# Product matmuls that read their moving rows alternately from two halves, in a fp32 decoder trunk

## What is computed

```python
def _swiglu(h, w_gate, w_up, w_down):
    return (jax.nn.silu(h @ w_gate) * (h @ w_up)) @ w_down

def _shortconv_mixer(h, w_in, conv_w, w_out):
    proj = h @ w_in
    b_gate, c_gate, u = jnp.split(proj, 3, axis=-1)
    z = c_gate * u
    ...
    return (b_gate * y) @ w_out

def reference(x, ...):
    for i in range(DEPTH):
        j = i // N_MIXERS
        if i % N_MIXERS == 0:
            x = x + _dsa_mixer(_rmsnorm(x, attn_norm[j]), ...)
        else:
            x = x + _shortconv_mixer(_rmsnorm(x, conv_norm[j]), ...)
        x = x + _swiglu(_rmsnorm(x, ffn_norm[i]), w_gate[i], w_up[i], w_down[i])
    return x
```

## Time and profile before

| | us |
|---|---|
| median of two runs | 2096.52 (2096.46 to 2096.58) |
| span of the profiled execution | 2096.4 |
| TensorE busy | 2081.3 (99%) |
| weight loads busy | 1729.7 (83%) |
| VectorE busy | 1725.3 (82%) |
| ScalarE busy | 1177.2 (56%) |

### The profile page before, as it was taken

How to read it: one execution, slowest core, us unless ns; L and a number is a source line. 1 busy time by engine, 2 the same in 40 slices (tenths; PEclk the granted TensorE clock), 3 DMA queues, 4 the chain that set the end, 5 groups by cost and what they waited for, 6 DMA issues and landing times.

```text
span 2096.4 us, 28772 instructions
## 1 busy us (share of the span) xinstructions
PE 2081.3 (99%) x9675; PEld 1729.7 (83%) x9675; DVE 1725.3 (82%) x1968; ACT 1177.2 (56%) x1428; POOL 118.3 (6%) x131
## 2 busy tenths in 40 slices
PE   8999999999999999999999999999999999999999
PEld 7888878788888888888888888888888888888887
DVE  5887757999999997876788877579999999978666
ACT  5456555665566564554465555466655665645443
POOL 0001000001000000000000000000010000000000
PEclk9999999999999999999999999999999999999999
DMA  7555456777777777667667666567777777767674
GB/s 230 152 145 152 158 171 192 223 224 227 228 226 220 231 219 215 216 202 215 211 196 211 204 203 196 190 196 222 224 226 229 225 221 230 221 213 216 204 220 147
DMA packets 251616, 432.33 MB, mean 206 GB/s; under 512 B 16912, under 2 KB 58000, under 8 KB 251536
## 3 DMA queue, kind: packets, MB, share of 16 engines
q1 hardware_dynamic: 233824, 399.23, 58.8%
q0 software_dynamic: 16848, 30.68, 8.7%
q10 hardware_dynamic: 864, 1.37, 0.2%
HBM read 429.12 MB, written 2.10 MB: 206 GB/s over the span
## 4 chain that ended last, share of the span: by engine, by line
PE 96%; DVE 2%; ACT 1%; issue 1%; DMA 0%; ACTq 0%; DVEq 0%; SPq 0%
PE ps L774 24%; PE ps L776 24%; PE ps L775 24%; PE ps L520 6%; PE ps L551 4%; PE ps L549 4%; PE ps L550 4%; PE ps L525 3%; PE ps L584 2%; DVE w_lo L1393 1%; PE ps L702 0%; PE ps L640 0%; ACT w_hi L1006 0%; PE ps L711 0%; PE ps L692 0%
## 5 line engine op out<-in xcount | busy, mean ns | idle before, releaser
L1393 DVE TENSOR_TENSOR w_lo<-stage,w_hi 128x1024 fp32r<-128x1024 f32 x748 | 902.3, 1222 | 232.4 <-ACT w_hi L1006 228.4
L1006 ACT ACTIVATE w_hi<-stage 128x1024 fp32r<-128x1024 f32 x748 | 772.7, 1055 | 536.6 <-PE ps L776 365.5
L774 PE MATMUL ps<-w_hi,xs 128*128 128x512 f32 x1122 | 439.4, 392 | 0.3
L776 PE MATMUL ps<-w_hi,xs 128*128 128x512 f32 x1122 | 437.0, 389 | 0.0
L775 PE MATMUL ps<-w_lo,xs 128*128 128x512 f32 x1122 | 436.6, 389 | 0.0
L774 PEld LDWEIGHTS ps<-w_hi,xs 128*128 128x128 f32 x1122 | 210.6, 188 | 44.3 <-DVE gated L1699 1.1
L776 PEld LDWEIGHTS ps<-w_hi,xs 128*128 128x128 f32 x1122 | 210.6, 188 | 44.1
L775 PEld LDWEIGHTS ps<-w_lo,xs 128*128 128x128 f32 x1122 | 210.7, 188 | 42.9
L774 PE MATMUL ps<-w_hi,hs 128*128 128x512 f32 x584 | 227.6, 390 | 0.0
L776 PE MATMUL ps<-w_hi,hs 128*128 128x512 f32 x584 | 227.2, 389 | 0.0
L775 PE MATMUL ps<-w_lo,hs 128*128 128x512 f32 x584 | 227.2, 389 | 0.0
(11 more groups left out here) (226 smaller groups left out, 2824.7 us busy)
## 6 DMA issues: line engine op xcount, KB each, us to landing
stage<-in_w_gate SPq DMA_DIRECT2D x176, 512.0 KB, 4.0
stage<-in_w_up SPq DMA_DIRECT2D x176, 512.0 KB, 4.9
stage<-in_w_down SPq DMA_DIRECT2D x176, 512.0 KB, 4.9
stage<-in_conv_w_in SPq DMA_DIRECT2D x96, 512.0 KB, 4.8
stage<-in_attn_w_in SPq DMA_DIRECT2D x48, 512.0 KB, 3.8
stage<-in_w_gate POOLq DMA_DIRECT2D x86, 256.0 KB, 5.6
stage<-in_attn_w_out SPq DMA_DIRECT2D x32, 512.0 KB, 4.8
stage<-in_conv_w_out SPq DMA_DIRECT2D x32, 512.0 KB, 4.8
```

Of the source, the lines that this page charges most:

```text
L774: pe.matmul(ps[:, bank, :], hi, b_hi, start=start, stop=False)
L776: return pe.matmul(ps[:, bank, :], lo, b_hi, start=False, stop=stop)
L1006: nc.scalar.activation(w_hi[:, j % RING, :], stage[:, at, :], ACT.Copy).then_inc(hi_done, 1)
L1393: tt(w_lo[:, p, :], stage[:, stage_at(first + j), :], f32(w_hi[:, p, :]), ALU.subtract).then_inc(lo_done, 1)
```

## The change

Each of the helper's three matmuls reads its moving operand in another order and writes its sums in the same other order. The 512 elements are taken as two halves of 256. The read takes 16 elements of the first half, then 16 of the second half, then the next 16 of the first, and so on to the end. The written PSUM columns are permuted alike, so each sum lands in the column where it was before.

```diff
             def product(bank, x_of, b_hi, b_lo, start, stop):
 
+                def woven(ap):
+
+                    return ap.rearrange("p (r o i) -> p o r i", r=2, i=16)
+
                 hi, lo = x_of
-                pe.matmul(ps[:, bank, :], hi, b_hi, start=start, stop=False)
-                pe.matmul(ps[:, bank, :], hi, b_lo, start=False, stop=False)
-                return pe.matmul(ps[:, bank, :], lo, b_hi, start=False, stop=stop)
+                sums_of = woven(ps[:, bank, :])
+                pe.matmul(sums_of, hi, woven(b_hi), start=start, stop=False)
+                pe.matmul(sums_of, hi, woven(b_lo), start=False, stop=False)
+                return pe.matmul(sums_of, lo, woven(b_hi), start=False, stop=stop)
```

## The result

The changed kernel takes 2184.72 us (median of two runs, 2184.1 to 2185.33) against 2096.52 us before: a ratio of 1.0418, with a 95% interval of 1.04 to 1.0435. It is slower by 88.2 us. The prediction said 2096.5 us, and its range ended at 2166.

The account below looks back on a forecast made before the run. TensorE was taken as the bound, through the distance between matmul starts. Instructions, moving read, PSUM write and stall change were each put at 0, so 6753 x 0 left 2096.5 us, with a range of 2022 to 2166.

Parts of the forecast that it names:

- What bounds the kernel: TensorE, busy 99% of the span; the helper's 6753 matmuls start 0.2267 us apart, so one nanosecond each is 6.75 us.
- The moving read ... I take 0: In the helper's matmuls, 31 jumps per moving read were taken to cost 0, with 10.3 ns as the upper bound.
- 591 and 592 ns: Median durations of half-pace 512-column matmuls at lines 717 and 720/722, reading one run and four runs; used to price jumps.
- 0.33 ns "at most": Upper price of one jump in the moving read, from 1 ns for 3 jumps; 31 jumps would be 10.3 ns.
- Inside a run of 16 elements nothing differs from now: Reason given for a free reordered moving read and for the no-change forecast, chance 0.48.
- The PSUM write at 0: Writing the helper's sums to PSUM with jumps was taken to cost 0, bounded above by 10.3 ns.
- Rival C: Gapped PSUM writes run at half pace: 429 ns between matmul starts, 3460 us; chance 0.03.
- What the 13.3 ns were: Each matmul's time beyond its 512 columns, read as moving read and weight load stalling each other in SBUF; assumed unchanged.
- wide and narrow matmuls seemed to lose 14 ns each: In the projection before, 512- and 256-column matmuls both lost 14 ns, so the loss was tied to the weight load.
- Rival B: Jumps cost in the moving read or PSUM write: 10.3 ns a matmul, 70 us, 2166 us; chance 0.22 including an unsettled stall.
- Rival A: The stall between moving read and weight load shrinks, 11 ns less a matmul, 2022 to 2040 us; chance 0.27.

Follow-up runs that it names:

- e1: The changed kernel with only the moving read reordered and the PSUM write in plain order; 2184.76 us, 1.0413 of the kernel before.
- e5: The changed kernel with the runs of 16 taken from four quarters in turn instead of two halves; 2126.70 us, 1.0134 of the kernel before.
- e6: The kernel before with one unused 64-byte tile ahead of xs, shifting the stationary tiles; 2141.94 us, 1.0207 of the kernel before.
- m1: Bare kernel without the trunk's computation, forty matmul forms with read, write or both reordered; plain 227 ns, read in runs of 16 from two halves 240 ns.
- m3: Bare kernel without the trunk's computation, forms varying the moving read's steps and column count; runs of 16 every 64 elements 242 ns, every 80 227 ns.
- e2: The changed kernel with only the PSUM write reordered and the moving read in plain order; 2097.98 us, 0.9999 of the kernel before.
- m2: Bare kernel without the trunk's computation, forms varying the stationary block's start and width; plain read 227 to 233 ns by start, 231 ns with 2 stationary columns.
- e4: The changed kernel, read and write, with runs of 64 elements instead of 16; 2097.95 us, 1.0002 of the kernel before.
- e3: The changed kernel, read and write, with runs of 32 elements instead of 16; 2163.21 us, 1.0307 of the kernel before.

## Why the prediction was wrong

**What bounds the kernel**: right. TensorE's distance between starts is the whole story, 6753 matmuls are the right count, and 6.75 us a nanosecond is the right rate: e1 to e5 follow it, and e6 does with the 1152 of `stream_rows` counted in.

**"The moving read ... I take 0"** is the step that failed, the term that should have been 13.3 ns. It rested on the earlier trace rows, 591 and 592 ns for one run and for four. Those are float32 matmuls at half pace, and m1 shows that at half pace even runs of 16 cost nothing (25.91 us both times). Besides, their runs of 128 elements are whole multiples of 256 bytes, which cost nothing at full pace either. The nearest row of the trace was blind to the effect in two ways. I saw the first difference and still used the row to weigh the chances. Nor was 0.33 ns "at most" a bound: two medians, each rounded to 1 ns, can lie nearly 2 ns apart, which is 0.67 ns a jump and 20 ns for 31, more than the 13.3 that came.

**"Inside a run of 16 elements nothing differs from now"** is beside the point: what the runs of m3 show to count is the order of the 64-byte places. Plain order visits 0, 1, 2, 3 of each 256 bytes; two halves in turn visit 0, 0, 1, 1, 2, 2, 3, 3. That the second order costs 13.3 ns is measured; why it does is not shown.

**The PSUM write at 0**: right (e2, and m1 down to runs of 4). Rival C falls with it. The rule that the Trainium skill gives in "PSUM — Partial Sum Buffer" (specifications), that any non-contiguous pattern slows matmuls significantly, does not hold for these forms: the measurement is 226.7 ns for runs of 4, 8, 16 and longer. The prediction called the part on memory cachelines in "Advanced Engine Details and Errata" milder; that part of the Trainium skill has the same sentence beside the one that I took from it, and m1 speaks against it there as well.

**What the 13.3 ns were**: wrong in the main, right in a detail. I took them for a meeting with the weight load. m2 and m3 show them with 2 stationary columns, and growing with the columns. The argument from the earlier trace rows, where wide and narrow matmuls seemed to lose 14 ns each, was misleading, because 128 weights and 256 columns side by side have their own 120 ns (m1), where 2 weights leave 113. The detail is that the two reads do affect each other by their addresses (m2, e6). "TensorE: Matmul & The Clock Gate" of the Trainium skill, in its part on issuing a matmul, has the weights' read take nothing from the moving one. The runs do not agree: the 128-column load at another start costs 6.6 ns a matmul in m2, and 44 us in e6.

**Rival B** named the right side. Its aside, "would already be 31 x 0.42 = 13 ns", even has the number, and I left it outside the range because the earlier trace rows seemed to cap a jump at 0.33 ns. Its mechanism, a cycle for each jump, is refuted by e4 and by the row of m3 with one run every 80. **Rival A** did not happen in any order tried.

**What stays open**: why plain order still loses a sixteenth of its pace, and how the machinery behind the places works. "The next place is free" does not give the 231 ns of four quarters (three steps to the same place, then one to the next) beside the 239 of eight parts and the 240 of two halves, nor the 228 to 237 ns of the two halves from last to first. The bare kernels tabulate the prices; they don't explain them.

## What to carry to other kernels

Let an fp32r matmul with 512 moving columns read its moving rows in address order, or in whole pieces of 256 bytes (64 and 128 elements were tried, from starts that are multiples of 256 bytes); a reorder in 64-byte pieces cost 2 to 7% of the matmul in most of the orders tried (one every 80 elements was free, and falling order came down to 1% at two of four starts), while runs of 16 on the PSUM side, in bf16 or in plain float32 were free. Keep the starts of moving and stationary tiles equal modulo 256 bytes: one 64-byte tile in the wrong place cost 44 us here and changed no instruction. Before costing an access pattern from the nearest row, ask whether that row runs at the same pace, and if a bare loop of thirty matmuls can be run, trust it: the times worked out from three of its numbers (e3, e5, e6) came back from the trunk within 2 us.

## What the runs showed of the hardware

- fp32r, 512 columns, 128 weights: 226.7 ns a matmul at best, against 215.8 for bf16 and 429 for each of float32's two passes. That is a sixteenth over the columns' own time.
- The pace of the read depends on the order of 64-byte places within 256 bytes (m3): next place 227 ns, two on 240, three on 238, the same 242. Mixed orders are not the mean of these: two halves in runs of 16 take 240, and the same from last to first 228 to 237, by the start of the weights (m2).
- PSUM writes in runs of 4 to 128 columns cost nothing (m1; e2 in the trunk).
- Start addresses: stationary block 0, 16, 32, 48, 64 elements on gives 227, 233, 233, 229, 227 ns (m2). With 2 stationary columns it is 232 ns at every start tried (m3).
- When matmuls at another difference of starts follow each other, the distance takes some matmuls to settle: five in e6.
- A moving read of every second element takes 451 ns and of every fourth 461 (m3), where the columns alone would be 213.
